# Prompt rows of four experts gathered and transposed in one piece, sample rows transposed ahead of the down projection, and another third of the weight splits on GpSimd

## The reference, cut to what matters

```python
def expert_choice_ffn(h, w_router, w_gate, w_up, w_down):
    ...
    aff = jax.nn.softmax((t @ w_router).astype(jnp.float32), axis=-1)
    cap = max(1, EC_CAPACITY * n_tok // N_EXPERTS)
    gate, idx = lax.top_k(aff.T, cap)
    xe = jnp.take(t, idx, axis=0)
    hid = jax.nn.silu(jnp.einsum("ecd,edf->ecf", xe, w_gate)) * jnp.einsum("ecd,edf->ecf", xe, w_up)
    ye = jnp.einsum("ecf,efd->ecd", hid, w_down) * gate[..., None].astype(h.dtype)
    out = jnp.zeros_like(t).at[idx.reshape(-1)].add(ye.reshape(-1, D))
```

## Time and profile before

| | us |
|---|---|
| median of 3 runs (2651.76 to 2651.93) | 2651.77 |
| span of the profiled execution | 2647.7 |
| PE busy with matmuls, share of the span | 2414.7 (91%) |
| PE busy with weight loads | 2089.8 (79%) |
| DVE busy | 1235.3 (47%) |
| ACT busy | 981.3 (37%) |
| POOL busy | 444.2 (17%) |
| start of product 0 of expert 2 | 1858.99 |
| start of product 0 of expert 3 | 1914.22 |

### The profile page before, as it was taken

One profiled execution on the slowest core, in us unless ns is written; L12 is line 12 of the kernel. 1 busy time (PEld: TensorE's weight loads), 2 busy tenths in 40 slices (PEclk: granted clock), 3 DMA queues, 4 the chain that ended last, 5 costly groups with the idle time before them and its releaser, 6 DMA issues. The chain is left out here.

```text
span 2647.7 us, 38172 instructions
## 1 busy us (share of the span) xinstructions
PE 2414.7 (91%) x14495; PEld 2089.8 (79%) x14495; DVE 1235.3 (47%) x1813; ACT 981.3 (37%) x1644; POOL 444.2 (17%) x306
## 2 busy tenths in 40 slices
PE   5999998999799999999899798069999999999997
PEld 4876665666688888888788687069999999999997
DVE  6334345445423320000244434956666666666663
ACT  6333333434500011211300222135565555655653
POOL 0001101110200000000000000023434434344342
PEclk7999998998999999999899899579999999999998
DMA  5300000001011112222344443268788887888872
GB/s 167 104 24 25 17 24 17 17 25 40 2 47 40 40 31 83 90 89 89 104 153 146 170 159 116 90 196 257 235 257 250 261 256 233 258 249 264 254 234 64
DMA packets 328236, 342.67 MB, mean 129 GB/s; under 512 B 11856, under 2 KB 308816, under 8 KB 327632
## 3 DMA queue, kind: packets, MB, share of 16 engines
q1 hardware_dynamic: 315280, 309.96, 37.3%
q0 software_dynamic: 12864, 31.46, 4.5%
HBM read 297.35 MB, written 44.04 MB: 129 GB/s over the span
## 5 line engine op out<-in xcount | busy, mean ns | idle before, releaser
L1977 PE MATMUL bank_pair<-tokens_hi_lo,ehi 128*128 128x320 f32 x2048 | 534.0, 347 | 1.1 <-DVE tokens_hi_lo L1843 1.1
L1978 PE MATMUL bank_pair<-tokens_hi_lo,elo 128*128 128x160 f32 x2048 | 483.9, 236 | 0.0
L1978 PEld LDWEIGHTS bank_pair<-tokens_hi_lo,elo 128*128 128x128 f32 x2048 | 392.5, 192 | 0.0
L1977 PEld LDWEIGHTS bank_pair<-tokens_hi_lo,ehi 128*128 128x128 f32 x2048 | 385.7, 188 | 1.2 <-issue 1.2
L1778 ACT ACTIVATE ehi<-eraw 128x2048 fp32r<-128x2048 f32 x192 | 366.2, 1907 | 10.8 <-DMA eraw<-in_w_eg 7.9
L1836 DVE TENSOR_TENSOR elo<-eraw,ehi 128x2048 fp32r<-128x2048 f32 x144 | 329.2, 2287 | 82.7 <-ACT ehi L1778 82.7
L1754 POOL TENSOR_TENSOR elo<-eraw,ehi 128x2048 fp32r<-128x2048 f32 x47 | 224.8, 4783 | 388.2 <-ACT ehi L1778 388.2
L1977 PE MATMUL bank_pair<-hidden_hi_lo,ehi 128*128 128x320 f32 x1024 | 271.6, 348 | 19.1 <-DVE hidden_hi_lo L1849 19.1
L1978 PE MATMUL bank_pair<-hidden_hi_lo,elo 128*128 128x160 f32 x1024 | 241.4, 236 | 0.0
L1977 PEld LDWEIGHTS bank_pair<-hidden_hi_lo,ehi 128*128 128x128 f32 x1024 | 191.9, 187 | 23.4 <-DVE hidden_hi_lo L1849 22.1
L1206 PE MATMUL bank_pair<-hT_hi,whi 128*128 128x512 f32 (+1 forms) x576 | 204.0, 354 | 1.2 <-PEq L1036 1.2
(11 more groups left out here) (245 smaller groups left out, 4365.0 us busy)
## 6 DMA issues: line engine op xcount, KB each, us to landing
eraw<-in_w_eg SPq DMA_DIRECT2D x64, 1024.0 KB, 7.3
eraw<-in_w_eu SPq DMA_DIRECT2D x64, 1024.0 KB, 5.4
eraw<-in_w_ed SPq DMA_DIRECT2D x64, 1024.0 KB, 5.3
raw<-in_w_in SPq DMA_DIRECT2D x64, 512.0 KB, 4.1
scratch_g<-sig SPq DMA_DIRECT2D x24, 640.0 KB, 3.4
sig<-scratch_g SPq DMA_DIRECT2D x24, 640.0 KB, 3.9
xt<-in_x SPq DMA_DIRECT2D x10, 512.0 KB, 4.6
scratch_m<-acc SPq DMA_DIRECT2D x8, 640.0 KB, 4.9
```

The source lines that it names most:

```text
L1977: nc.tensor.matmul(out, wh, moving[:, k, :], start=(k == 0), stop=False)
L1978: ins = nc.tensor.matmul(out[:, HI], wl, moving[:, k, HI], start=False, stop=(k == KD - 1))
```

## The change

Four things change in the expert stage.

- **Prompt rows in groups.** The prompt rows of four experts (4 x 32 = 128 rows) are gathered by one DMA into `x_rows_p`, transposed by eight 128x128 transposes into the PSUM bank pair that also takes the results (`prompt_rows`, after product 9 of every fourth expert), and copied by ACT to SBUF as `x_prompt_T` (`prompt_copy`). Each expert then takes its 32 columns from there: the third split of the tokens (`x_split(e, 2)`) reads SBUF and writes the prompt's part of `xp`.
- **Sample rows.** The eight transposes of the next expert's sample rows stand together and ahead of product 8 instead of after products 9 and 10, in two batches that fill the two other banks. ACT and DVE split them where they did, at j = 10.
- **Splits.** POOL makes the low parts of chunks 1, 5 and 9 instead of 3, 7 and 11; DVE makes those of 3, 7 and 11. Both index copy and gather stand one iteration earlier in the code (j = 2 instead of 3), which is the same place behind POOL's split.
- **Bodies.** `run_experts` now writes out groups of four bodies: four, a loop over two groups of four, and four.

Before the first expert DVE makes four more copies of the prompt's indices and lays out the index columns of a group.

```diff
-    xg = [place("x_rows_s", [P, D]), place("x_rows_p", [CAP_P, D])]
+    xg = [place("x_rows_s", [P, D]), place("x_rows_p", [P, D])]
+    GROUPS = NEXP // PACK
+    xpT = at("x_prompt_T", [P, KD, P], F32, HT)
...
+    idx_rep = place("idx_repeated", [NEXP, PACK, CAP_P])
+    idx_c = [place("idx_cols_s", [CAP_S, NEXP], U32), place("idx_cols_p", [P, GROUPS], U32)]
     g_cur = [place("gate_s", [CAP_S, 1]), place("gate_p", [P, 1])]
...
-    XB = ((0, 3), (3, 6), (6, 8))
+    xp_tr = sem("prompt_rows_transposed")
+    xp_cp = sem("prompt_rows_copied")
+    XB = ((0, 4), (4, 8))
+    HALF = 2
     AHEAD = 4
+    def by_pool(j):
+        return j % 4 == 1
     def wait_lo(eng, e, j):
-        if j % 4 == 3:
+        if by_pool(j):
             eng.wait_ge(e_lo_p, 3 * e + j // 4 + 1)
         else:
-            eng.wait_ge(e_lo_d, 9 * e + j - j // 4 + 1)
+            eng.wait_ge(e_lo_d, 9 * e + j - (j + 2) // 4 + 1)
     def run_experts(eng, body):
-        body(0, False, True)
-        body(1, True, True)
-        with eng.Fori(2, NEXP - 1) as e:
-            body(e, True, True)
-        body(NEXP - 1, True, False)
+        for i in range(PACK):
+            body(i, i, 0, i > 0, True)
+        with eng.Fori(1, GROUPS - 1) as g:
+            for i in range(PACK):
+                body(PACK * g + i, i, g, True, True)
+        for i in range(PACK):
+            body(NEXP - PACK + i, i, GROUPS - 1, True, i < PACK - 1)
...
-            def gather(e):
+            def gather(e, group):
                 pool.wait_ge(ig_ready, e + 1)
-                wait_apart(pool, x_tr, 3 * e, pool_passed)
-                for s in range(2):
-                    nc.gpsimd.indirect_dma_start(xg[s][:], None, scratch_t[:],
-                                                 bass.IndirectOffsetOnAxis(ap=ig_cur[s][:], axis=0)).then_inc(
-                        gathered[s], 16)
+                wait_apart(pool, x_tr, HALF * e, pool_passed)
+                nc.gpsimd.indirect_dma_start(xg[0][:], None, scratch_t[:],
+                                             bass.IndirectOffsetOnAxis(ap=ig_cur[0][:], axis=0)).then_inc(
+                    gathered[0], 16)
+                if group is not None:
+                    wait_apart(pool, xp_tr, group, pool_passed)
+                    nc.gpsimd.indirect_dma_start(xg[1][:], None, scratch_t[:],
+                                                 bass.IndirectOffsetOnAxis(ap=ig_cur[1][:], axis=0)).then_inc(
+                        gathered[1], 16)
...
-                    if jn % 4 == 3 and (after or jn < NCH):
+                    if by_pool(jn) and (after or jn < NCH):
                         pool.wait_ge(e_hi, NCH * e + jn + 1)
                         nc.gpsimd.tensor_tensor(elo[jn % NES][:], eraw[jn % NER][:], ehi[jn % NES][:].bitcast(F32),
                                                 ALU.subtract).then_inc(e_lo_p, 1)
                     if j == 0 and before:
                         scatter(e - 1)
-                    if j == 3 and after:
-                        gather(e + 1)
-            pool.wait_ge(e_hi, 4)
-            nc.gpsimd.tensor_tensor(elo[3][:], eraw[3][:], ehi[3][:].bitcast(F32), ALU.subtract).then_inc(e_lo_p, 1)
+                    if j == 2 and after:
+                        gather(e + 1, g + 1 if i == PACK - 1 else None)
+            pool.wait_ge(e_hi, 2)
+            nc.gpsimd.tensor_tensor(elo[1][:], eraw[1][:], ehi[1][:].bitcast(F32), ALU.subtract).then_inc(e_lo_p, 1)
...
-            def x_split(e, b):
-                act.wait_ge(x_tr, 3 * e + b + 1)
-                k0, k1 = XB[b]
-                src = bank[4 + b % 2][:, 0:(k1 - k0) * CAP].rearrange("p (k t) -> p k t", t=CAP)
-                nc.scalar.activation(xp[:, k0:k1, HI], src, ACT.Copy).then_inc(x_hi, 1)
+            def prompt_copy(group):
+                act.wait_ge(xp_tr, group + 1)
+                wait(act, x_lo, 3 * PACK * group)
+                nc.scalar.activation(xpT[:].rearrange("p k t -> p (k t)"),
+                                     pair_bank[:].rearrange("p a b -> p (a b)"), ACT.Copy).then_inc(xp_cp, 1)
+            def x_split(e, b, i, group):
+                if b < HALF:
+                    act.wait_ge(x_tr, HALF * e + b + 1)
+                    k0, k1 = XB[b]
+                    src = bank[4 + b][:].rearrange("p (k t) -> p k t", t=CAP_S)
+                    nc.scalar.activation(xp[:, k0:k1, 0:CAP_S], src, ACT.Copy).then_inc(x_hi, 1)
+                else:
+                    act.wait_ge(xp_cp, group + 1)
+                    nc.scalar.activation(xp[:, :, CAP_S:CAP], xpT[:, :, CAP_P * i:CAP_P * (i + 1)],
+                                         ACT.Copy).then_inc(x_hi, 1)
...
                     if after and j == 10:
-                        x_split(e + 1, 0)
-                        x_split(e + 1, 1)
+                        x_split(e + 1, 0, nxt, g + (nxt == 0))
+                        x_split(e + 1, 1, nxt, g + (nxt == 0))
                     if after and j == 11:
-                        x_split(e + 1, 2)
+                        if nxt == 0:
+                            prompt_copy(g + 1)
+                        x_split(e + 1, 2, nxt, g + (nxt == 0))
...
+                else:
+                    nc.vector.tensor_tensor(xp[:, :, CAP + CAP_S:2 * CAP], xpT[:, :, CAP_P * i:CAP_P * (i + 1)],
+                                            xp[:, :, CAP_S:CAP].bitcast(F32), ALU.subtract).then_inc(x_lo, 1)
...
-                    if jn % 4 != 3 and (after or jn < NCH):
+                    if not by_pool(jn) and (after or jn < NCH):
                         lo(e, jn)
...
+                nc.vector.tensor_copy(idx_rep[:, k, :], idx_r[1][:])
...
+            nc.vector.tensor_copy(idx_c[0][:], bank[4][:, 0:NEXP])
+            for k in range(PACK):
+                rows = slice(CAP_P * k, CAP_P * (k + 1))
+                nc.vector.tensor_copy(idx_c[1][rows, :], bank[5][rows, k:NEXP:PACK])
             for s in range(2):
-                nc.vector.tensor_copy(idx_c[s][:], bank[4 + s][0:CAPS[s], 0:NEXP])
...
-            def x_rows(e, b):
-                if b == 0:
-                    for s in range(2):
-                        pe.wait_ge(gathered[s], 16 * e + 16)
-                    if isinstance(e, int) and e == 0:
-                        pe.wait_ge(cols_ready, 1)
-                wait(pe, x_lo, 3 * e + (b == 2))
-                k0, k1 = XB[b]
-                for k in range(k0, k1):
-                    at_k = (k - k0) * CAP
-                    f = slice(k * P, (k + 1) * P)
-                    nc.tensor.transpose(bank[4 + b % 2][:, at_k:at_k + CAP_S], xg[0][:, f], ident[:])
-                    ins = nc.tensor.transpose(bank[4 + b % 2][:, at_k + CAP_S:at_k + CAP], xg[1][:, f],
-                                              ident[0:CAP_P, 0:CAP_P])
-                ins.then_inc(x_tr, 1)
-            def y_back(e, s):
+            def x_rows(e):
+                pe.wait_ge(gathered[0], 16 * e + 16)
+                if isinstance(e, int) and e == 0:
+                    pe.wait_ge(cols_ready, 1)
+                wait(pe, x_lo, 3 * e)
+                for b, (k0, k1) in enumerate(XB):
+                    for k in range(k0, k1):
+                        ins = nc.tensor.transpose(bank[4 + b][:, (k - k0) * CAP_S:(k - k0 + 1) * CAP_S],
+                                                  xg[0][:, k * P:(k + 1) * P], ident[:])
+                    ins.then_inc(x_tr, 1)
+            def prompt_rows(group):
+                pe.wait_ge(gathered[1], 16 * group + 16)
+                wait(pe, y_rdy, 2 * (PACK * group - 1))
+                for k in range(KD):
+                    ins = nc.tensor.transpose(pair_bank[:, k // 4, (k % 4) * P:(k % 4 + 1) * P],
+                                              xg[1][:, k * P:(k + 1) * P], ident[:])
+                ins.then_inc(xp_tr, 1)
+            def y_back(e, s, copied):
                 if s == 0:
                     pe.wait_ge(summed, NCH * e + NCH)
+                    if copied is not None:
+                        pe.wait_ge(xp_cp, copied)
...
                     if j == 8:
+                        if after:
+                            x_rows(e + 1)
                         pe.wait_ge(h_lo, 4 * e + 3)
                         product(e, j, range(6))
                         pe.wait_ge(h_lo, 4 * e + 4)
                         ins = product(e, j, range(KD))
                     ins.then_inc(mm5, 1)
                     if before and j in (0, 1):
-                        y_back(e - 1, j)
-                    if after and j == 9:
-                        x_rows(e + 1, 0)
-                        x_rows(e + 1, 1)
-                    if after and j == 10:
-                        x_rows(e + 1, 2)
+                        y_back(e - 1, j, g + 1 if i == 0 else None)
+                    if after and i == PACK - 1 and j == 9:
+                        prompt_rows(g + 1)
```

## The result

| | before | after |
|---|---|---|
| median, us | 2651.77 (4 runs, 2649.4 to 2651.93) | 2628.44 (4 runs, 2626.72 to 2629.55) |
| span of the profiled execution | 2647.7 | 2625.0 |
| start of product 0 of expert 0 | 1746.72 | 1744.45 |
| a usual expert | 55.2 | 53.6 |
| DVE busy | 1235.3 | 1260.5 |

The ratio of after to before is 0.9912, with a 95% interval of 0.9898 to 0.9926: 23 us faster, where 22.3 were forecast (2629.5 us). A product is 16 pairs of matmuls, not 32 as said above: the trace has 3072 rows with `ehi` for 192 products.

What follows compares the result with a forecast made beforehand. PE, busy 91% of the span, was taken as the bound. Terms -38.4 - 22.7 + 18 + 18 + 1.8 + 0.5 + 0.5 = -22.3 us took 2651.8 to 2629.5 us; 8-in-10 range 2613 to 2649.

Steps and rivals of the forecast that it cites:

- Transposes: At 15 hand-overs on PE: eight sample transposes (0.79 us) replace token transposes of 2.54 + 0.81 us; -2.56 each, -38.4 us.
- rival of dear transposes: Transposes cost 0.2 us each, so the saving is 0.8 smaller 15 times: 2641 us; chance 0.07.
- Wait in product 8: PE's wait there for the hidden values' low part goes whole: 1.42 us, 16 times, -22.7 us.
- Wait before product 5: POOL's split of chunk 5 waits out one DVE split, so product 5 starts 1.2 us later in 15 experts: +18.
- not held up: Rival: DVE's split does not delay POOL's; wait before product 5 is 0.3 instead of 1.2 us: 2616 us; chance 0.15.
- one instruction later: Rival: POOL also sits out the hidden values of j = 3; wait before product 5 is 2.4 us: 2648; chance 0.11.
- POOL starves: Rival: POOL gets the port only after DVE's split of chunk 8; product 5 waits 5.3 us: 2691 us; chance 0.06.
- Wait before product 0: DVE's list ends late, at 1912.0, so the next expert's product 0 is 1.2 us late, 15 times: +18 us.
- Groups: Three times, eight prompt transposes between products 9 and 10 shift DVE's work: +0.6 us each, +1.8 us.
- Before expert 0: Before the first product: transposes save 3 us, prompt's own put 2 back, gather +1, DVE's copies +0.6; sum +0.5 us.
- Code: PE's loop grows from one body to four; one jump back may cost up to 1.2 us: +0.5 us.

## Why the prediction was right, step by step

Of the 22.7 us between the two spans, each is found: product 0 of expert 0 is 2.3 earlier; expert 0 takes 53.15 instead of 57.03; fourteen experts save 1.62 each, 22.7 in all; three group hand-overs give back 2.0 and the loop's turn 5.7; the tail saves 1.6.

The forecast also carries over that the median is 4.1 us above the span. Only 1.6 to 1.7 of it lies around the program, as the four runs after the change show against their own spans; the rest is most likely that the profiled execution is the fastest one, of 2649.40 us. Nothing hangs on it, since the forecast is a difference.

*Transposes, -2.56 an expert.* Right: 0.79 us for eight, and 2.6 less by the starts of products 7 to 11. The rival of dear transposes falls with that row, and the sorted ones show why the old ones were dear.

*Wait in product 8, -1.42.* Right: product 8 takes 4.17 us instead of 5.53.

*Wait before product 5, +1.2.* Right in size (product 4 plus the restart in product 5 cost 1.17 more) and in cause. The port is held for one instruction, so the rivals "not held up", "one instruction later" and "POOL starves" all fall; the run with VectorE's split later splits the wait into 0.8 for the port and 0.3 for the scatter.

*Wait before product 0, +1.2.* Right: product 11 takes 5.31 instead of 4.19 us, by DVE's list as worked out, the collision of chunk 14's split with POOL included (0.40). The rows at the end of expert 2 show it, and putting the token split first takes it away.

*Groups, +1.8.* 2.0 measured.

*Before expert 0, +0.5.* The span is 3.4 shorter here, but only a third of that belongs to the term. 1.2 us is there before anything that was changed: the stretch of lower clock ahead of the stage starts at 1642.24 instead of 1643.47, PE's transposes of the chosen indices at 1725.30 instead of 1726.45. In three variants with the same program up to there these transposes start at 1725.77, 1726.03 and 1727.96, so executions differ by as much. Another 1.1 is the first product, 5.83 instead of 6.93 us, the higher clock being granted 4.6 us earlier (1748.06); the kernel before with sorted transposes has that as well (1749.60, 5.94 us), so the grouping is not what it takes.

1.1 us is left, between these transposes and product 0 (20.27 before, 19.15 after). DVE's copies add 0.7 (0.6 forecast), and from PE's first prompt transpose on it is 1.0 shorter (about 1 forecast: 3 saved, 2 put back). The step that failed is the gather: +1 forecast, but from POOL's first gather to that transpose it takes 10.69 us instead of 11.47. The term put the longer prompt gather in front. It did not see that the sample's gather would get the port sooner:

```profile
1728.44 2.06 POOL L1738 DMA_INDIRECT x_rows_s<-scratch_t,idx_gather_s  x1 [62.22 <-issue]
1730.80 1.84 POOL L1743 DMA_INDIRECT x_rows_p<-scratch_t,idx_gather_p  x1 [0.30 <-issue]
```

It now sits out one of DVE's two splits instead of both the earlier trace rows, and the sample's transposes no longer wait for the prompt's rows; the prompt's do:

```profile
1739.13 1.97 PE L1997 MATMUL bank_pair<-ident,x_rows_p 128*128 128x128 f32 x8 [0.94 <-DMA x_rows_p<-scratch_t,idx_gather_p]
```

All nine kernels with the grouping have 2.05 or 2.06 us for the first gather, the two variants of the kernel before 4.25. Why, no run tells.

*Code, +0.5.* Mis-sized: +5.7 in the traces; without the loop the median is 4.6 lower. The bound was taken from an earlier jump of PE that cost 1.2 us; this one stops PE and ACT for over 4 us, DVE waits for ACT, and a stretch at the lower clock follows. The Trainium skill, Runtime: NRT & Kernel Launch, section Instruction fetch mechanics, says that a taken branch whose target is outside the window of code at hand forces a fetch before execution goes on. The turn after the change agrees, with its three packets of code and its 4.75 us of idle time. The twelve turns of the loop before cost nothing, and from 1920 to 2560 us its two code queues bring no packet at all, so its body of a quarter the length was at hand. Packets alone are no stop: from 2186 to 2560 us, where the changed kernel's code runs straight on, q8 brings 22, and PE waits for none. Over the runs with this loop the turn costs 4 to 10 us, but nothing in the run with GpSimd on chunks 3, 7, 11 and the token split last, where PE has to wait 3.1 us at the same place anyway.

*The tail, no term.* Product 0 of expert 15 to the end is 1.6 us shorter. 0.3 of it lies in the expert (0.2 by its two terms); 1.3 lie behind the landing of the last scatter. All nine kernels with the grouping have 21.6 to 21.8 us from product 11 of expert 15 to the end, the three without it 23.0 to 23.1. The cause stays open.

The last three errors cancel (-3.9, +5.2 and -1.3 against what was forecast). That the total came within about 1 us of the forecast is luck to that extent; what was right for its reasons is the 1.6 us that an expert saves.

What the forecast did not weigh is how much its parts depend on each other. Against 2651, the splits alone give +2 us, the grouping alone +36, and both -23. Moving the splits is worth nothing by itself and 59 us beside the grouping, because the grouping turned a token split with one SBUF input into one with two, right beside POOL's split of chunk 3. The same splits with the token split first show it: 2600.3 us, 87 less.

## What to carry to other kernels

When an edit moves an operand of a VectorE instruction from PSUM to SBUF, look at what GpSimd runs beside it: 0.4 us can become 4.6. Weigh the parts of a change in pairs, and put the short instruction that TensorE waits for ahead of the long split in both helpers' lists; here that one reordering gave 16 us beyond the change, and one sorted loop by itself 22. A loop with a long body can pay at its turn: here 4 to 10 us, unless the engine has to wait there anyway.

## What was not expected of the hardware

- Sixteen transposes of two shapes cost 3.35 us in turn and 2.14 sorted (1.50 and 0.64 us); eight of one shape cost 0.79.
- After idle times of PE of about 1 us the granted clock stays at its higher level. With one of 3.1 to 3.2 us in each expert it is 1.2 GHz for 6.8 us in 13 of 15 cases, for 3.4 in one and not at all in one. The loop's turn brings 3.4 us of it in one run and 13.7 in another.
- A loop body of four experts stops PE for 4.75 us and ACT for 4.63 us at its turn, one of a single expert does not.
- DVE and POOL stand still for the other's instruction when both have two SBUF inputs: a token split takes 4.56 us instead of 0.41, and a POOL split that arrives inside a DVE split starts when that ends (6.02 us recorded instead of 5.18).
